# Transposing cached tokens on VectorE in 32x32 blocks, from pages loaded in quarters

## The reference

```
def _nsa_compress(kv_pad, cmp_pos, w1, w2):
    chunks = kv_pad[:, :, :2].reshape(b, n_chunks, CMP_STRIDE, 2, NSA_KV_HEADS, NSA_HEAD_DIM)
    w1 = w1.reshape(2, CMP_LEN, NSA_HEAD_DIM, CMP_HIDDEN)
    pos_bias = jnp.einsum('rld,rlde->re', cmp_pos, w1)
    pa = jnp.einsum('bnlrkd,rlde->bnrke', chunks, w1[:, :CMP_STRIDE])
    pb = jnp.einsum('bnlrkd,rlde->bnrke', chunks, w1[:, CMP_STRIDE:])
    hidden = jax.nn.gelu(pa[:, :-1] + pb[:, 1:] + pos_bias[:, None, :])
    out = jnp.einsum('bnrke,ref->bnrkf', hidden, w2)
```

## Time and profile before

| | us |
|---|---|
| median of three runs | 2550.19 (2540.56 to 2556.83) |
| the profiled execution, its span | 2552.3 |
| PE busy | 2406.9 (94%) |
| DVE busy | 1308.8 (51%) |
| ACT busy | 735.5 |
| POOL (GpSimd) busy | 26.4 |
| compression of layer 0, from 159.7 to 309.4 | 149.7 |

### The profile page before, as it was taken

The page is one execution under the profiler, slowest core; times in us unless marked ns, Lnnn a source line. Parts: engine busy times, 40 slices in busy tenths (PEclk is TensorE's granted clock), DMA queues, the critical chain, the costliest instruction groups (busy, mean ns, idle before and its releaser), DMA issues. The chain is left out here.

```text
span 2552.3 us, 45434 instructions
## 1 busy us (share of the span) xinstructions
PE 2406.9 (94%) x19182; PEld 2040.0 (80%) x19182; DVE 1308.8 (51%) x2332; ACT 735.5 (29%) x1763; POOL 26.4 (1%) x26
## 2 busy tenths in 40 slices
PE   8989988899999889999999898999999998979998
PEld 6668865699986767999888766899985786648998
DVE  2257384265552373666443285366631865535565
ACT  2125373221022342210232293221021445522200
POOL 0000000000000010000000010000000000000000
PEclk9999899999999979999999857999999997889999
DMA  9997616965644317666433255656671865293440
GB/s 346 307 241 166 210 49 214 350 229 213 245 160 144 99 56 283 212 251 223 154 132 134 68 150 195 233 204 256 217 207 66 181 177 159 71 321 122 172 170 22
DMA packets 287343, 472.71 MB, mean 185 GB/s; under 512 B 14956, under 2 KB 105149, under 8 KB 286662
## 3 DMA queue, kind: packets, MB, share of 16 engines
q1 hardware_dynamic: 272370, 456.04, 54.8%
q10 hardware_dynamic: 14770, 13.76, 1.7%
HBM read 448.72 MB, written 38.04 MB: 191 GB/s over the span
## 5 line engine op out<-in xcount | busy, mean ns | idle before, releaser
L631 PE MATMUL PS<-hT,ring 128*128 128x132 f32 x2048 | 249.7, 277 | 6.6 <-DVE hT L756 4.2
L631 PEld LDWEIGHTS PS<-hT,ring 128*128 128x128 f32 x2048 | 238.3, 190 | 11.9 <-issue 11.2
L631 PE MATMUL PS<-mT,arena 128*128 128x132 f32 x1536 | 184.6, 276 | 0.0
L631 PEld LDWEIGHTS PS<-mT,arena 128*128 128x128 f32 x1536 | 178.7, 190 | 0.0
L2687 PE MATMUL PS<-hT,ring 128*128 128x264 f32 x768 | 172.7, 386 | 0.1
L2687 PEld LDWEIGHTS PS<-hT,ring 128*128 128x128 f32 x768 | 145.1, 190 | 24.9 <-issue 0.4
L768 DVE TENSOR_TENSOR arena<-arena,PS 128x264 f32<-128x264 f32 x224 | 89.7, 427 | 130.8 <-PE PS L631 129.6
L715 ACT ACTIVATE arena<-arena 128x528 f32<-128x528 f32 x64 | 41.1, 642 | 312.1 <-DVE arena L768 312.1
L631 PE MATMUL PS<-arena,ring 128*128 128x132 f32 x1024 | 126.9, 277 | 0.0
L631 PE MATMUL PS<-hT,arena 128*128 128x132 f32 x1024 | 125.7, 276 | 0.0
L631 PE MATMUL PS<-mT,ring 128*128 128x132 f32 x1024 | 125.7, 276 | 0.0
(11 more groups left out here) (490 smaller groups left out, 4364.0 us busy)
## 6 DMA issues: line engine op xcount, KB each, us to landing
arena<-in_w_ada SPq DMA_DIRECT2D x36, 2048.0 KB, 12.1
ring<-in_w_mlp_in SPq DMA_DIRECT2D x32, 2048.0 KB, 8.7
ring<-in_w_mlp_out SPq DMA_DIRECT2D x32, 2048.0 KB, 8.1
ring<-in_w_ada SPq DMA_DIRECT2D x12, 2048.0 KB, 19.9
ring<-in_ssd_w_in SPq DMA_DIRECT2D x12, 2048.0 KB, 7.9
ring<-in_nsa_w_in SPq DMA_DIRECT2D x10, 2048.0 KB, 9.5
arena<-in_cache_nsa_kv SPq DMA_DIRECT2D x64, 256.0 KB, 10.5
ring<-in_cache_nsa_kv SPq DMA_DIRECT2D x64, 256.0 KB, 8.0
```

The source lines that it names most:

```text
L631: ins = nc.tensor.matmul(PS[:, bank, at:at + HALF], lhs[:, k, p * 128:(p + 1) * 128], rhs[:, k, :], start=opens and k == 0, stop=closes an ...
```

## The change

The pages are fetched in quarters, so that a chunk's positions are spread over four blocks of 32 partitions, and DVE transposes 32x32 blocks within them. PE's transposes, their PSUM banks and both sets of copies are gone. In detail:

- `quarter_pages` (line 950) issues four DMAs of 16x2x512 (64 KB) per page, each to 16 neighbouring partitions, 64 per group. SP issues 48 of groups 1 to 3 (`SYNC_PAGES`), GpSimd 16 (`POOL_PAGES`); group 0 is issued by GpSimd alone in the projection stage, behind `h_sample`. The page numbers are read for two pages at a time.
- `nsa_cmp_w1` is loaded by sixteen DMAs per r (`compress_weights`), its rows in the new order. The position table is laid out to match and loaded by four DMAs in place of one.
- DVE's `turn(m)` is one transpose of 128x1024 (128x128 for the prompt), and waits for `product_made` of four steps before; it is issued one step ahead of `differences(m)`.
- The difference of an even step is one subtraction of 1024 elements on DVE. In odd steps DVE subtracts 512 and GpSimd the other 512 (`pool_step`), and PE waits for both.
- GpSimd's program: the pages of group 1, subtractions of steps 1, 3, 5, 7, pages of group 2, subtractions 9 to 15, pages of group 3, subtractions 17 to 31.
- The pair product alternates between two PSUM banks.

```diff
-        def chunk_pages(sp, L, g, G, samples=(0, 1)):
-            for b in samples:
-                for n in range(0, PAGES, 4):
-                    numbers = page_numbers(sp, [(2 * g + b) * PAGES + q for q in range(n, n + 4)])
-                    for q, number in zip(range(n, n + 4), numbers):
-                        page = cache_chunks[bass.ds(number + L * N_PHYS, 1), :, :, 0:2, :]
-                        fetched[g % 2].on(sp.dma_start(G[g % 2][b][q:128:PAGES],
-                                                       page.rearrange("g c t r n -> (g c) t (r n)")), 16)
+            return [P(2 * PAGES, 2 * KV * HD), ring[:, 0:2].rearrange("p s k n -> p (s k) n")]
+
+        def quarter_pages(engine, kind, signals_, L, g, G, items):
+            for n in range(0, len(items), 2):
+                b, q0 = items[n]
+                numbers = page_numbers(engine, [(2 * g + b) * PAGES + q for _b, q in items[n:n + 2]], kind)
+                for number, (b, q) in zip(numbers, items[n:n + 2]):
+                    for i in range(4):
+                        part = cache_quarters[bass.ds(number + L * N_PHYS, 1), i, :, :, 0:2, :]
+                        row = 32 * i + 16 * (q % 2)
+                        signals_[g % 2].on(engine.dma_start(G[g % 2][row:row + 16, 8 * b + q // 2 * 2:8 * b + q // 2 * 2 + 2, :],
+                                                            part.rearrange("g c t r n -> (g c) t (r n)")), 16)
+
+        POOL_PAGES = [(1, q) for q in range(4, PAGES)]
+        SYNC_PAGES = [(0, q) for q in range(PAGES)] + [(1, q) for q in range(4)]
...
+        def compress_weights(sp, done, dst, L, r):
+            src = a["nsa_cmp_w1"][L, r].rearrange("(h i c d) e -> i d h c e", h=4, i=4, c=4)
+            to = dst.rearrange("p (h c e) -> p h c e", h=4, c=4)
+            for h in range(4):
+                for i in range(4):
+                    done.on(sp.dma_start(to[32 * i:32 * i + 32, h], src[i, :, h]), 16)
...
+            def gp_part(gp):
+                gp.wait_ge(h.h_sample.sem, h.h_sample.at(1))
+                quarter_pages(gp, mybir.EngineType.Pool, fetched_pool, L, 0, G, SYNC_PAGES + POOL_PAGES)
...
-                    chunk_pages(sp, L, 1, G)
+                    sync_pages(sp, L, 1, G)
...
                     for g in (2, 3):
-                        sp.wait_ge(pt_ready.sem, pt_ready.at(8 * (g - 1)))
-                        chunk_pages(sp, L, g, G)
+                        sp.wait_ge(turned.sem, turned.at(8 * (g - 1)))
+                        sync_pages(sp, L, g, G)
...
+                @block.gpsimd
+                def _(gp):
+                    pool_pages(gp, L, 1, G)
+                    for m in range(1, 4 * cached, 2):
+                        gp.wait_ge(turned.sem, turned.at(m + 1))
+                        j = m % 4
+                        pool_step.on(nc.gpsimd.tensor_tensor(delta[:, j, 0:512], x[:, j, 0:512], x[:, j, 512:1024],
+                                                                 ALU.subtract))
+                        if m in (7, 15):
+                            pool_pages(gp, L, m // 8 + 2, G)
...
+                    def turn(m):
+                        n, j = divmod(m, 4)
+                        g, r = order[n]
+                        if r == 0 and j == 0:
+                            loaded_group(v, g)
+                        if m >= 4:
+                            v.wait_ge(product_made.sem, product_made.at(m - 3))
+                        if n < cached:
+                            ins = nc.vector.transpose(columns_of(j), rows_of(G[g % 2], r, j))
...
+                        turned.on(ins)
...
                     def differences(m):
                         j = m % 4
...
-                        nc.vector.tensor_tensor(whole(before[:, j, :]), even, odd, ALU.subtract)
-                        nc.vector.tensor_tensor(chunk_rows(y, 0, 3), chunk_rows(even, 1, 4), chunk_rows(odd, 0, 3), ALU.subtract)
-                        differed.on(nc.vector.tensor_tensor(last_row(y, 3, 0), last_row(even, 0, 1), last_row(odd, 3, 0),
-                                                            ALU.subtract))
+                        v.wait_ge(turned.sem, turned.at(m + 1))
+                        a = j % 2
+                        differed.on(nc.vector.tensor_tensor(delta[:, j, 512 * a:].rearrange("p (a n) -> p a n", n=512),
+                                                            shifted(j)[:, a:], bc(x[:, j, 512:1024], 1, 2 - a), ALU.subtract))
```

More of the change, by code:

```diff
@@ L254, in hybrid_trunk @@
         fetched = [signal(f"fetched{i}") for i in range(2)]
+        fetched_pool = [signal(f"fetched_pool{i}") for i in range(2)]
         ada_loaded = [signal(f"ada_loaded{j}") for j in range(2)]
@@ L1023, in sp_part @@
                     issue(sp, n0 + 5)
[L1024 to L1033, removed]
+                compress_weights(sp, loaded2, mT_flat[:, 0:2048], L, 0)
+                issue(sp, n0 + (13 if first else 5))
                 sp.wait_ge(in_taken.sem, in_taken.at(np_))
@@ L1416, in _ @@
                     position(0)
-                    for j in range(4):
-                        turn(0, j)
-                    pe.wait_ge(loaded.sem, loaded.at(16))
                     for n in range(len(order)):
+                        if n == 1:
+                            pe.wait_ge(loaded.sem, loaded.at(256))
                         for j in range(4):
@@ L1451, in differences @@
                     def differences(m):
                         j = m % 4
-                        v.wait_ge(pt_taken.sem, pt_taken.at(m + 1))
-                        v.wait_ge(pt_taken2.sem, pt_taken2.at(m + 1))
-                        even, odd, y = halves(j)[:, 0], halves(j)[:, 1], whole(after[:, j, :])
-                        nc.vector.tensor_tensor(whole(before[:, j, :]), even, odd, ALU.subtract)
-                        nc.vector.tensor_tensor(chunk_rows(y, 0, 3), chunk_rows(even, 1, 4), chunk_rows(odd, 0, 3), ALU.subtract)
@@ L1471, in _ @@
+                    turn(1)
+                    differences(0)
                     sum_weights(0)
                     position(0)
-                    for m in range(4 * len(order)):
+                    for m in range(1, last):
                         n, j = divmod(m, 4)
-                        if j == 3 and 0 < n <= cached:
-                            add_pairs(n - 1)
-                        v.wait_ge(pt_ready.sem, pt_ready.at(m + 1))
-                        for dst, src in regroup(m, 0):
-                            ins = nc.vector.tensor_copy(dst, src)
-                        pt_taken.on(ins)
+                        if m + 1 < last:
+                            turn(m + 1)
@@ L2616, in rest @@
                 return hT, 1, first
-            return parts, rest
+            return parts, rest, None
         dt_raw = signal("dt_raw")
@@ L3271, in _ @@
                         tables_in.on(act.dma_start(rows[r:r + n, i, :], src), 16)
+                    for c in range(4):
+                        dst = rows[16 * c:16 * c + 16, 5, :].rearrange("p (i d) -> p i d", i=4)
+                        tables_in.on(act.dma_start(dst, positions[c]), 16)
                     tables_in.on(act.dma_start(relb, a["rel_bias"]), 16)
```

203 lines of the change are left out of this document (94 added, 109 removed).

## The result

The changed kernel takes 2587.02 us (median of four, 2576.74 to 2597.34), the kernel before 2553.51 (2540.56 to 2559.81). The ratio is 1.013, with a 95% interval of 1.0084 to 1.0176: slower by more than the noise, and by less than 2%. The forecast of 2592 was a ratio of 1.016. The profiled execution (2579.02 us) is one of the faster of the four.

What follows compares the result with a forecast made beforehand. The prediction took the compression stage to be bound by PE before, then paced by page transfers: 2552.3 + 36.6 for two compressions + 5 for group 0 = 2593.9, less 2.1 from profiled run to median, 2592 us; range 2524 to 2608.

Steps and rivals of the forecast that it cites:

- the 64 us at stake: Compression stage, bound by PE: removing its transposes frees some 32 us per stage, 64 in all, the most possible.
- Transfers at 111 GB/s, 37.8 us per group: Compression's page loads: quarter pages move at 111 GB/s, so a 4.19 MB group takes 37.8 us; +18.3 us per stage.
- rival 1: Compression's page loads: transfers or issues pace at 37 us per group, giving 2592 us; chance 0.43.
- case 1: Page loads pace at 37 us per group, 2592 us; its sign is a DMA share near 1 at 110 GB/s; chance 0.43.
- The row: Profile row behind the transfer price: DMAs to 16 contiguous partitions moved 111 GB/s at a share of 1.10.
- Issues at 0.62 us, 29.8 per group: SP's queue in the compression: 0.62 us per quarter page, 48 in 29.8 us; stage 152.0 us against 149.7.
- rival 2: Compression's page loads: SP's issues pace at 0.62 us each, total 2555 to 2560 us, no change; chance 0.27.
- The end of the stage: Behind the last cached product: removed prompt transposes shorten 15.9 us of prompt steps by 4.2; 4.4 of tail stay.
- VectorE's transpose: DVE's new transpose of 128x1024 per compression step: 1.22 us, between 0.61 and about 2.1.
- GpSimd's issues: GpSimd's quarter-page issues, sixteen per group: 1.14 us each, between 0.56 and 1.58.
- Rival 3: GpSimd's page issues, from 1.3 us each upwards, hold back its own subtractions: +13.4 us per stage, 2577; chance 0.10.
- Group 0, taken as 5 and bounded by 13.4: Layer 0's projection stage: GpSimd's load of group 0 collides with weight transfers, 0 to 13.4 us, taken as 5.

Runs made afterwards that it cites:

- ports8: Changed kernel with each quarter page spread over every second partition of its block of 32, same size and queues; 2635.72 us, ratio 1.0306.
- best: `halves8` with its first page half waiting for compression weights, and ScalarE issuing 16 of SP's 48 page DMAs per group and 8 key-page DMAs; 2635.27 us, ratio 1.0307.
- halves8: Changed kernel, layer 0's group 0 loaded by GpSimd in two halves at the old places, quarters on every second partition; 2559.59 us, ratio 1.0006.
- g0_wide: Changed kernel with group 0 loaded by GpSimd as 16 old-shape DMAs of 256 KB; span 2561.3 us, layer 0's compression starts at 176.9.
- key_pool: Changed kernel with 16 of the 32 key-page issues at the compression's end moved from SP to GpSimd; span 2583.2 us.

## Why the forecast's number was right and most of its sum was not

**The sum.** 2592 was forecast, 2587 measured; +36.6 for two compressions and +5 for group 0 were forecast, and the traces have +0.5 for the compressions and +31.6 for group 0. Errors of 36 us too much and 27 too little nearly cancelled. In spans, 2593.9 - 36.1 + 26.6 - 7.0 (the other stages) = 2577.4, the span of the profiled run; the median of the runs lies 8 us above that run's own 2579.02. That the number came out within 5 us was luck.

**What bounds the kernel, and the 64 us at stake**: right. PE lost 65 us of work. That the queues would take all of it back inside the compression was right too (151.0 us against 149.7), though not at the price that the forecast took.

**Transfers at 111 GB/s, 37.8 us per group** (rival 1, the forecast): this step failed. Pages moved at 147 GB/s at a share near 1, which is the sign of case 1 with the rate of neither case:

```profile
200.00:228.00 28.00, 17.53 (x61) 14.17 (x60) 22.42 (x28) 2.52 (x4) 13.50 (x19) 0.73 0.97 146
234.00:262.00 28.00, 21.87 (x109) 18.74 (x110) 21.88 (x18) 4.29 (x10) 6.86 (x4) 0.83 1.03 147
262.00:290.00 28.00, 26.15 (x142) 21.79 (x140) 23.89 (x20) 6.02 (x14) 16.96 (x21) 1.00 0.69 147
```

From group 1 to group 3 it is 292.15 - 234.60 = 57.6 us, 28.8 per group. The row was one microsecond long, with two DMAs to the same 16 partitions, and SP had already begun to issue its window copies behind them (at 2061.56). The quarters of a page go to four blocks; that they overlap in part would explain their higher rate, but no run tests it. That shape matters at all was right: `ports8` nearly halves the engines' time per byte (0.41 / 112 against 0.97 / 146). By the Trainium skill, "SBUF — State Buffer", section "Door 1: The DMA port swizzle", 16 neighbouring partitions give 104 GB/s, and spreading them over a block of 32 reaches twice the ports: the ratio agrees with `ports8`, the rate does not with 147.

**Issues at 0.62 us, 29.8 per group** (rival 2): measured 0.57 and 27.3 to 28.6. The stage was to be 152.0 and is 151.0 and 150.7. So this sum fits the compression, but that issues pace it is not shown: the transfers need as long (share 0.97 to 1.03 in two of three windows), and in `best`, with fewer issues on SP, the rate stayed the same up to 230 us. Nor was SP's queue back to back: group 3 waited for its buffer, and only groups 1 and 3 kept VectorE waiting (10.39 and 4.21 us, where 10 or more were expected at each of the later groups).

**The end of the stage**: I let the prompt's 4.2 us of transposes shorten it, from 15.9 + 4.4 to 16.1. It stayed 20.3, since SP's 32 key-page issues stood there (19.35 us before, 19.33 after, each beginning with the last cached product). I had not looked at SP's queue behind the last product.

**VectorE's transpose**, taken as 1.22: 1.95, inside the bounds and near the upper one. The last group took 29.9 us (292.15 to 322.06) in place of 27.2. A tile of 128 elements takes 0.40, so it is 1.73 ns per element and a small start; for the subtraction, (1220 - 690) / 512 = 1.04.

**GpSimd's issues**, taken as 1.14: 0.67. Rival 3 had no part, and the port lock that I cited for it has not lengthened an issue (507 to 647 ns in all 224). Its subtraction was taken as 1.27 and is 2.12 beside VectorE's difference:

```profile
261.27 1.20 DVE L1481 TENSOR_TENSOR ring<-arena 128x1024 f32<-128x1024 f32 x1
261.51 2.13 POOL L1356 TENSOR_TENSOR ring<-arena 128x512 f32<-128x512 f32 x1 [3.56 <-DVE arena L1469]
```

It starts at 261.51 and ends 1.17 us after VectorE's subtraction does (262.47), close to its time alone (1.27 in the earlier trace rows). Where VectorE's came second, at 204.35, its 512 elements took 1.38 us instead of 0.67. The Trainium skill, "SBUF — State Buffer", section "Who interferes with whom", has it that a VectorE instruction with two SBUF inputs contends with a GpSimd instruction that reads SBUF, and that the port pair they share is an exclusive lock; the trace agrees.

**Group 0, taken as 5 and bounded by 13.4**: 31.6. This is the other step that failed, and it carried the result. I reckoned with sums of bytes over the whole stage, as if any transfer could use any free time. But PE needs weight units in order, the ring holds four of them, and a lump of pages beside the next unit delays it: PE waited 25.8 us. After that the engines had time to spare (share 0.72 from 106 to 160 us). The shape that I priced for the later groups acts here as well: of the 25.4 us that `halves8` wins back, shape alone gives 12 and place alone 11. In layer 3, where a share of 0.43 was used before, the same loads cost nothing (86.9 us of projection before, 84.9 after). The Trainium skill, "DMA: Bandwidth & Descriptors", section "Issuing engines are not separate DMA queues", says that a second engine saves only the issue's time, because all DMAs run on the same 16 engines; `g0_wide` shows it: GpSimd had issued all 16 DMAs by 60.3 us, and SP's weight DMAs beside them stood for 14.09 and 18.47 us at the head of its queue.

## What to carry to other kernels

Where the DMA engines are full, ask of every transfer that is moved which one it will stand in front of, not how many bytes are free over the stage: a queue of its own takes bandwidth from the transfer that is needed next. And price a transfer's shape twice, in issue time and in the engines' time; here the spread shape nearly halves the second and nearly doubles the first on SP, and which one counts changes from stage to stage. Before counting work removed from an engine's end of a stage, look at all queues behind the last product.

## What was not expected of the hardware

- A quarter page to 16 neighbouring partitions takes 0.317 us to issue on SP, to every second partition 0.581; on GpSimd 0.507 and 0.504.
- VectorE's 32x32 block transpose of 128x1024 takes 1.95 us, also with the columns written in steps of four and eight; of 128x512 some 1.08.
- In `key_pool`, where the compression ends with DMA issues on GpSimd, the next stage begins 7.8 us after the last of them (7.5 in layer 3); after SP's last one it was 0.4.
- A DMA issue that takes 0.37 us in the kernel before stood for 23.07 us at the head of SP's queue beside the 64 page DMAs, and everything behind it on SP with it.
